# Feed-forward gate and up products: one product of 512 columns with the high weight part, a PSUM bank each

## The reference, cut to what matters

```
def swiglu(x, w_gate, w_up, w_down):
    return (jax.nn.silu(x @ w_gate) * (x @ w_up)) @ w_down

x = layer_norm(ALPHA_2 * x + 0.5 * swiglu(x, ffn1_gate[l], ffn1_up[l], ffn1_down[l]), ...)
```

## Time and profile before

| | us |
|---|---|
| median of three runs | 2454.69 |
| profiled execution | 2451.98 |
| its span | 2450.1 |
| PE in feed-forward part i = 0, from | 1355.73 |
| part i = 1, from | 1702.95 |
| part i = 2, from | 1898.18 |
| part i = 3, from | 2253.99 |

### The profile page before, as it was taken

The page is one execution under the profiler, slowest core; times in us unless marked ns, Lnnn a source line. Parts: engine busy times, 40 slices in busy tenths (PEclk is TensorE's granted clock), DMA queues, the critical chain, the costliest instruction groups (busy, mean ns, idle before and its releaser), DMA issues.

```text
span 2450.1 us, 32486 instructions
## 1 busy us (share of the span) xinstructions
PE 2217.7 (91%) x13534; PEld 1638.8 (67%) x13534; DVE 1116.8 (46%) x1616; ACT 753.5 (31%) x1154; POOL 129.0 (5%) x110
## 2 busy tenths in 40 slices
PE   7978997999896889988988999978999999878998
PEld 7874442443386844434433899878998999777997
DVE  4662221121358732221212655576556555677555
ACT  3432110111143221101111444443444444544443
POOL 0010000000002200000000000031000000031000
PEclk9989999999996799999999999988999999988999
DMA  9448999999951289999999746423554566323551
GB/s 294 136 145 330 420 420 421 417 420 421 387 174 35 85 332 421 420 420 417 420 421 400 244 164 211 160 69 104 189 184 166 186 204 203 124 70 104 189 186 56
DMA packets 231550, 622.81 MB, mean 254 GB/s; under 512 B 15456, under 2 KB 166944, under 8 KB 182112
## 3 DMA queue, kind: packets, MB, share of 16 engines
q1 hardware_dynamic: 225952, 604.99, 65.1%
q0 software_dynamic: 3040, 10.78, 1.3%
q10 hardware_dynamic: 2400, 4.83, 0.6%
HBM read 619.51 MB, written 1.05 MB: 253 GB/s over the span
## 4 chain that ended last, share of the span: by engine, by line
PE 41%; DMA 6%; DVE 4%; issue 2%; ACT 1%; POOL 1%; SPq 0%; DVEq 0%; POOLq 0%; ACTq 0%
PE bank L228 27%; PE bank L1486 9%; PE bank L1326 3%; DMA x_tok<-in_moe_w_up 1%; DMA wide_tables<-in_moe_w_up 1%; PE bank L1601 1%; DMA w_parts<-in_moe_w_up 1%; DMA ring<-in_moe_w_up 1%; DMA ring<-in_ffn_gate 1%; DVE w_low L429 1%; POOL mixT L1696 1%; DVE x_tok L674 0%; DVE x_tok L663 0%; DVE bn L652 0%; PE bank L469 0%
## 5 line engine op out<-in xcount | busy, mean ns | idle before, releaser
L429 DVE TENSOR_TENSOR w_low<-ring,w_high 128x1024 fp32r<-128x1024 f32 x364 | 442.7, 1231 | 375.9 <-ACT w_high L422 375.8
L228 PE MATMUL bank<-xT_high,w_high 128*128 128x256 f32 x1712 | 487.0, 284 | 19.8 <-DVE xT_low L491 12.0
L228 PE MATMUL bank<-xT_low,w_high 128*128 128x256 f32 x1712 | 485.2, 283 | 0.0
L228 PE MATMUL bank<-xT_high,w_low 128*128 128x256 f32 x1712 | 485.1, 283 | 0.0
L422 ACT ACTIVATE w_high<-ring 128x1024 fp32r<-128x1024 f32 x364 | 376.6, 1052 | 295.7 <-PE bank L228 274.7
L1326 PE MATMUL bank<-ring,arena 128*64 128x512 f32 x1344 | 339.2, 594 | 17.5 <-DMA wide_tables<-in_moe_w_gate 5.4
L228 PEld LDWEIGHTS bank<-xT_high,w_high 128*128 128x128 f32 x1712 | 329.0, 192 | 25.7 <-DVE xT_low L491 12.0
L228 PEld LDWEIGHTS bank<-xT_low,w_high 128*128 128x128 f32 x1712 | 329.1, 192 | 2.8
L228 PEld LDWEIGHTS bank<-xT_high,w_low 128*128 128x128 f32 x1712 | 329.1, 192 | 0.0
L1326 PE MATMUL bank<-w_parts,arena 128*64 128x512 f32 x768 | 260.8, 599 | 12.9 <-DMA w_parts<-in_moe_w_up 6.3
L1326 PEld LDWEIGHTS bank<-ring,arena 128*64 128x64 f32 x1344 | 111.0, 137 | 229.6 <-issue 220.9
(11 more groups left out here) (285 smaller groups left out, 3084.6 us busy)
## 6 DMA issues: line engine op xcount, KB each, us to landing
ring<-in_moe_w_gate SPq DMA_DIRECT2D x56, 1024.0 KB, 23.7
ring<-in_moe_w_up SPq DMA_DIRECT2D x56, 1024.0 KB, 22.2
ring<-in_moe_w_down SPq DMA_DIRECT2D x56, 1024.0 KB, 26.0
ring<-in_ffn_gate SPq DMA_DIRECT2D x44, 1024.0 KB, 5.5
ring<-in_ffn_up SPq DMA_DIRECT2D x44, 1024.0 KB, 5.4
ring<-in_ffn_down SPq DMA_DIRECT2D x44, 1024.0 KB, 5.3
w_parts<-in_moe_w_down SPq DMA_DIRECT2D x32, 1024.0 KB, 26.4
w_parts<-in_moe_w_gate SPq DMA_DIRECT2D x32, 1024.0 KB, 21.7
```

Of the source, the lines that this page charges most:

```text
L228: ins = e.matmul(out, lhs, rhs, start=first and i == 0, stop=last and i == len(parts) - 1)
L429: e.tensor_tensor(lo, src, hi.bitcast(F32), ALU.subtract).then_inc(*S.low.tell(key))
```

## The change

For each f, gate and up now get a bank each. In it, the high part of the weight meets both parts of x in one matmul of 512 columns (left half: by x high, right half: by x low), and the low part of the weight meets x high in one of 256 columns, added to the left half. x high and x low become one tile `x_parts`, read as two runs of 256 columns. The two halves are then summed outside of TensorE: ACT copies the left half to SBUF, DVE adds the right half, for gate and for up. Silu then works in place on the SBUF tile, and the multiplication takes both operands from SBUF.

```
     for f in range(FT):
-        bank = k.banks.open(e, B_BANKS, ("ffn", i, "hidden", f))
-        for half, name in enumerate(("gate", "up")):
+        for name in ("gate", "up"):
             key = ("ffn", i, name, f)
+            bank = k.banks.open(e, B_BANKS, ("ffn", i, name + " sum", f))
             _, hi, lo = split_views(k, key)
             e.wait_ge(*S.low[key])
-            mm(e, bank[:, half * T:(half + 1) * T], three([((hi[:, j, :], lo[:, j, :]), (k.xh[:, j, :], k.xl[:, j, :])) for j in range(KT)])
-               ).then_inc(*S.used.tell(key))
+            for j in range(KT):
+                e.matmul(pairs(bank[:, :]), hi[:, j, :], k.x_parts[:, :, j, :], start=j == 0, stop=False)
+                ins = e.matmul(bank[:, 0:T], lo[:, j, :], k.xh[:, j, :], start=False, stop=j == KT - 1)
+            ins.then_inc(*S.used.tell(key))
...
 def ffn_act(e, k, i):
     for f in range(FT):
-        for _ in range(2):
+        for name, out in (("gate", k.ffn_gate), ("up", k.ffn_hidden)):
             ffn_fill(e, k, i, n, n + 1, split_act)
             n += 1
-        bank = k.banks["ffn", i, "hidden", f]
-        e.wait_ge(*S.used["ffn", i, "up", f])
-        if f >= 2:
-            e.wait_ge(*S.ffn_low[i, f - 2])
-        e.activation(k.ffn_silu[:, f % 2, :], bank[:, 0:T], ACT.Silu).then_inc(*S.ffn_silu.tell((i, f)))
+            e.wait_ge(*S.used["ffn", i, name, f])
+            if f >= 2:
+                e.wait_ge(*S.ffn_low[i, f - 2])
+            e.activation(out[:, f % 2, :], k.banks["ffn", i, name + " sum", f][:, 0:T], ACT.Copy).then_inc(*S.ffn_first.tell((i, name, f)))
+        e.wait_ge(*S.dve_out["ffn", i, "gate sum", f])
+        e.activation(k.ffn_gate[:, f % 2, :], k.ffn_gate[:, f % 2, :], ACT.Silu).then_inc(*S.ffn_silu.tell((i, f)))
         e.wait_ge(*S.dve_out["ffn", i, "hidden", f])
...
 (ffn_dve)
     for f in range(FT):
-        for _ in range(2):
+        for name, out in (("gate", k.ffn_gate), ("up", k.ffn_hidden)):
             ffn_fill(e, k, i, n, n + 1, split_dve)
             n += 1
-        bank = k.banks["ffn", i, "hidden", f]
+            bank = k.banks["ffn", i, name + " sum", f]
+            e.wait_ge(*S.ffn_first[i, name, f])
+            e.tensor_tensor(out[:, f % 2, :], out[:, f % 2, :], bank[:, T:2 * T], ALU.add).then_inc(*S.dve_out.tell(("ffn", i, name + " sum", f)))
         e.wait_ge(*S.ffn_silu[i, f])
-        e.tensor_tensor(k.ffn_hidden[:, f % 2, :], k.ffn_silu[:, f % 2, :], bank[:, T:2 * T], ALU.mult).then_inc(*S.dve_out.tell(("ffn", i, "hidden", f)))
+        e.wait_ge(*S.dve_out["ffn", i, "up sum", f])
+        e.tensor_tensor(k.ffn_hidden[:, f % 2, :], k.ffn_gate[:, f % 2, :], k.ffn_hidden[:, f % 2, :], ALU.mult
+                        ).then_inc(*S.dve_out.tell(("ffn", i, "hidden", f)))
...
-    k.xh, k.xl = (sb(name, [P, KT, T], F32R) for name in ("xT_high", "xT_low"))
+    k.x_parts = sb("xT_parts", [P, 2, KT, T], F32R)
+    k.xh, k.xl = (k.x_parts[:, i, :, :] for i in range(2))
```

More of the change, by code:

```diff
@@ L1489, in ffn_pe @@
     for f in range(FT):
-        bank = k.banks.open(e, B_BANKS, ("ffn", i, "hidden", f))
-        for half, name in enumerate(("gate", "up")):
+        for name in ("gate", "up"):
             key = ("ffn", i, name, f)
+            bank = k.banks.open(e, B_BANKS, ("ffn", i, name + " sum", f))
             _, hi, lo = split_views(k, key)
             e.wait_ge(*S.low[key])
-            if f == 0 and half == 0:
+            if f == 0 and name == "gate":
                 x_ready(e, k, n, 1)
-            mm(e, bank[:, half * T:(half + 1) * T], three([((hi[:, j, :], lo[:, j, :]), (k.xh[:, j, :], k.xl[:, j, :])) for j in range(KT)])
-               ).then_inc(*S.used.tell(key))
+            for j in range(KT):
+                e.matmul(pairs(bank[:, :]), hi[:, j, :], k.x_parts[:, :, j, :], start=j == 0, stop=False)
+                ins = e.matmul(bank[:, 0:T], lo[:, j, :], k.xh[:, j, :], start=False, stop=j == KT - 1)
+            ins.then_inc(*S.used.tell(key))
         if f >= FFN_LAG:
@@ L2330 @@
            "norm_loaded", "mix_high", "squares", "mean_square", "root", "pool_out", "router_loaded", "selected", "route_step", "ffn_done", "ffn_silu",
-           "ffn_high", "ffn_low", "decayed_k", "token_high", "token_low", "params_loaded", "wide_loaded", "masks_loaded", "masks_made", "out_stored")
+           "ffn_high", "ffn_low", "ffn_first", "decayed_k", "token_high", "token_low", "params_loaded", "wide_loaded", "masks_loaded", "masks_made", "out_stored")
 OVER_SIGNALS = ("selected", "product", "expert", "act_out", "dve_out")
@@ L2423, in tiles_and_signals @@
     k.mixT = sb("mixT", [P, KT, T])
-    k.xh, k.xl = (sb(name, [P, KT, T], F32R) for name in ("xT_high", "xT_low"))
-    k.x_tok_high, k.x_tok_low = (flat(t[:, :, :]).rearrange("p (b k d) -> p b k d", b=NB, k=KT) for t in (k.xh, k.xl))
+    k.x_parts = sb("xT_parts", [P, 2, KT, T], F32R)
+    k.xh, k.xl = (k.x_parts[:, i, :, :] for i in range(2))
+    k.x_tok_high, k.x_tok_low = (flat(t).rearrange("p (b k d) -> p b k d", b=NB, k=KT) for t in (k.xh, k.xl))
     part_slots = [sb(f"w_parts{i}", [P, SLOT]) for i in range(PARTS)]
@@ L2468, in tiles_and_signals @@
     k.arena = Arena(arena, nc.alloc_sbuf_tensor_at("arena_rounded", [P, words], F32R, offset=arena_at), words)
-    k.ffn_silu, k.ffn_hidden = (pairs(arena[:, 2 * T * i:2 * T * (i + 1)]) for i in range(2))
+    k.ffn_gate, k.ffn_hidden = (pairs(arena[:, 2 * T * i:2 * T * (i + 1)]) for i in range(2))
     k.hid_high, k.hid_low = (nc.alloc_sbuf_tensor_at(f"hidden_{x}", [P, HIDDEN, T], F32R, offset=arena_at + 4 * T * (4 + HIDDEN * i))
@@ L2477, in tiles_and_signals @@
      S.norm_loaded, S.mix_high, S.squares, S.mean_square, S.root, S.pool_out, S.router_loaded, S.selected, S.route_step, S.ffn_done, S.ffn_silu,
-     S.ffn_high, S.ffn_low, S.decayed_k, S.token_high, S.token_low, S.params_loaded, S.wide_loaded, S.masks_loaded, S.masks_made, S.out_stored
+     S.ffn_high, S.ffn_low, S.ffn_first, S.decayed_k, S.token_high, S.token_low, S.params_loaded, S.wide_loaded, S.masks_loaded, S.masks_made, S.out_stored
      ) = k.signals = [signal(name) for name in SIGNALS]
```

## The result

The changed kernel takes 2442.77 us (median of six runs, 2438.83 to 2445.87), the kernel before 2455.68 us beside it; the ratio is 0.9943 with a 95% interval of 0.9933 to 0.9954. One of the six runs of the kernel before took 4430.51 us and is not in the ratio. The forecast was 2442.3 us. The profiled execution took 2440.75 us, with a span of 2438.8 us, 11.3 us less than before.

A forecast was written before the change was run, and what follows sets the result against it. PE's matmul starts were taken to bound the feed-forward parts; 1408 steps of 8.8 ns save 12.4 us, ACT and DVE cost nothing, so 2454.7 - 12.4 = 2442.3 us. Range: 2438 to 2447 us (0.65), 2430 to 2456 for 8 in 10.

The forecast's parts named there:

- PE bounds the parts, and only the starts of matmuls count: Feed-forward parts: time is number of matmuls by distance of starts, until ACT's and DVE's extra work uses up its slack.
- The product, 8.8 ns a step: Gate and up, per feature block: three narrow matmuls (359.4 ns) become wide plus narrow (350.6); 1408 steps save 12.4 us.
- the 0.23 us that I had made a sign: PE starts in gate and up: a distance from wide to narrow unlike 0.23 us would show the forecast wrong.
- The part on top is by the matmul, not the column: PE matmuls: time above columns, 13.1 ns narrow and 17.5 wide, is mostly per matmul; a merged pair saves one.
- The second run: Wide product's moving operand, two runs 8 KB apart: taken as free; bounded by 13.1 ns more, a 6 us loss.
- ACT and DVE cost nothing: Feed-forward tiles: added copies and sums, 0.78 us (ACT) and 0.84 us (DVE) per tile, are hidden by PE.
- the slack at the end: Last tile of a part: low part of down 21 comes about 0.45 us later, leaving 0.7 of 1.16 us.
- Busy sums, 69 and 74 us: Over 88 tiles f: ACT busy about 69 us more and DVE about 74 us more.
- No gain: Rival: the wide product costs two narrow ones, 2453 to 2456 us; chance 0.13 together with the 2.5 ns rule's 2451.
- slower by the second run: Rival: the wide product's second run restarts the stream; with 13.1 ns for it, 2461 us; chance 0.07.
- A bigger gain: Rival: a narrow matmul behind a wide one costs 106.7 ns, the step 337.5, 31 us go: 2424 us; chance 0.10.
- By order: Rival: ACT's or DVE's chain exceeds the slack at each part's end, losing 3.6 us in all: 2446 us; chance 0.05.

The follow-up runs named there:

- e1: Changed kernel with the wide product again two narrow ones; banks, copies and sums stay: 2455.31 us, ratio 1.0001 to the kernel before.
- e2: Changed kernel with the wide product reading x high of two adjacent feature blocks as one run of 512 columns: 2442.47 us, one run.
- e5: Changed kernel with each added ACT copy and DVE sum issued twice: 2450.00 us, one run.
- e6: Changed kernel with each added ACT copy and DVE sum issued five times: 2668.81 us, one run.
- e3: Changed kernel with eight wide, then eight narrow products, for gate and for up: 2439.45 us, ratio 0.9937 to the kernel before.
- e8: Changed kernel without the narrow products (low by high not computed), wide ones alone: 2290.05 us, one run.
- e9: e7 with each tile's 12 down matmuls ordered by product first, changing the output bank each time: 2440.03 us, ratio 0.9938 to the kernel before.
- e7: Changed kernel with wide for gate and up, then narrow for both, in each tile f: 2439.38 us, ratio 0.9924 to the kernel before.
- e4: Changed kernel with products in the order wide, wide, narrow, narrow: 2440.57 us, ratio 0.9945 to the kernel before.

## Why the prediction was right

- **PE bounds the parts, and only the starts of matmuls count.** Right: 178 of 178 us busy, and e1, with ACT's and DVE's new work but the old matmuls, has the old time (ratio 1.0001).
- **The product, 8.8 ns a step.** Right in kind and a little small: undisturbed parts gained 3.5 us where 22 x 16 x 8.8 = 3.1 were said, about 10 ns a step. I had priced the wide product by the down rows, 230.8 ns. The runs show that down is a disturbed stream: undisturbed, a wide matmul costs 226.7 ns and a narrow one 119.8, both some 13 ns above their columns. Mixed one by one, as the change does it, a step costs 347 ns in one kind of tile (230 and 117), which is no more than the two undisturbed prices together (346.5), and 353 in the other, where wide to narrow is 233 to 241 ns and no longer the 0.23 us that I had made a sign. The mean, 350, met my 350.6 though neither kind of step was made up as I said; that is luck too.
- **"The part on top is by the matmul, not the column."** Shown, and more cleanly than the rows of before could: 13.4 ns at 512 columns and 13.1 at 256. The Trainium skill ("TensorE: Matmul & The Clock Gate", "Back-to-back issue gap") states columns by 2.4 GHz plus 2.5 ns for an isolated gap, and says that in a stream of weight loads and matmuls both set the spacing. These streams have a load for each matmul; 2.5 ns is too small for them, while the form, columns and a constant, agrees.
- **The second run.** Free (e2). The bound of 13.1 ns against the change was right to be kept and came to nothing.
- **ACT and DVE cost nothing.** Right, in the idle time of 0.70 us (0.7) and the slack at the end of 0.64 us (0.7) as well. ACT's sum for a tile without down, 3.61 us, should have been 3.66 by its own prices (Silu at 417 ns); nothing hangs on it. e5 and e6 put the limit between twice and five times the added work.
- **Busy sums, 69 and 74 us.** Measured 52 and 66, since instructions of one engine overlap (0.1 us for the copy and Silu above).
- **The rivals.** "No gain" and "slower by the second run" fell with the measured rounds and with e2. "A bigger gain" asked for 106.7 ns behind a wide one; in the changed kernel the starts give 112 to 120 at full clock. "By order" fell with the waits.
- **What I had not foreseen** is the half-clock stretch of 3.4 us, which took back 1.6 us and made the sum fit; without it the parts would have gained 14.0 us.

**Open:** what disturbs a wide matmul. Wide ones are seen disturbed behind narrow ones (e3) and behind down (e8); excluded are the order of the banks and of the stationary pieces in down (e9), the number of runs (e2) and ACT's and DVE's extra work (e5: the same two rounds). Why down is slow by itself was not found, nor what picks the faster or the slower kind of tile. What down reads, weights as the moving operand and the hidden tile as the stationary one, was not tested.

## What to carry to other kernels

Price a matmul by the distance of starts in a full stream, and look for a stream that is undisturbed before you read its fixed part. Where both products of one stationary piece fit one bank, merging them saves one fixed part (13 of 360 ns in undisturbed streams, 10 on average in this kernel), a gain that counts only where the matmul stream is the bound and where the sums lie under it; e1 undoes one half of such a change and tells in one run which half pays. When widths must be mixed, try them in long groups: here that avoided the slower kind of tile and no more, and it moved the release of the split weights, which cost 0.4 us at the end of each part (e7). And compare rounds before totals, where the stages ahead vary by more than the gain.

## What the runs showed of the hardware

- Wide F32R matmuls (128x512) started 226 or 227 ns apart undisturbed (e3, e7), narrow ones (128x256) 120, each with a load of a stationary piece. Down's wide ones took 2.77 to 2.80 us for twelve and 232.8 ns each in a run of 36.
- Taken in turn, wide and narrow settled into one of two patterns, 347 or 353 ns a step. A pattern lasted through five tiles where nothing stood between them (27.82 us in the changed kernel, 28.34 in part i = 0 of e5), and each tile behind a down was in the other one than the tile ahead of it.
- A moving operand in two runs 8 KB apart cost no more than one run: rounds of 8.35 and 8.42 us either way (e2).
- The order of the same 32 matmuls in a tile behind down made 5.54 (e7) to 5.60 us (the mean of the changed kernel) of them: 1% of the stream.
- At the start of a part, behind short transposes and a wait of 1.5 us, PE had the full clock in most of the traces; in three (the changed kernel, e4 and e6, each in part i = 2) it ran the first 3.4 us near the half level (0.54 and 0.51 in the first two), which cost 1.6 us.
